# First tiles behind both norms of the second block taken from the unnormalised residual

## Chip, core and metric

The kernel runs on one core of one Trainium2 chip. The metric is the device time of one execution in microseconds (us). Three timed executions of the kernel before gave 1817.52 us as median (1816.81 to 1820.13).

## What is computed

Two transformer blocks in a row on a sequence of 512 tokens with 1024 channels, all in f32. The change touches the second block only:

```python
# second block; x is the first block's output behind its closing norm
shift1, scale1, gate1, shift2, scale2, gate2 = split(silu(c) @ w_ada + b_ada, 6)
h = rmsnorm(x, norm1_g) * (1 + scale1) + shift1
proj = h @ w_in                      # 24 tiles of 128 columns: "in2"
xc = causal_dwconv(x_rnn, conv_w, conv_b)          # tiles 0 to 9 of proj
...                                  # gated recurrence on xc, latent attention, merge
x = x + gate1 * (merged @ w_out)
h2 = rmsnorm(x, norm2_g) * (1 + scale2) + shift2
u = causal_dwconv(h2 @ w_up, ffn_conv_w, ffn_conv_b)   # 44 tiles: "up", tile m and tile 22+m are a pair
x = x + gate2 * ((silu(u_gate) * u_val) @ w_down)
```

With a scale s per channel, a factor r per token and a shift b per channel, (x * s * r + b) @ W is r * ((x * s) @ W) + b @ W. The last form needs r only behind the matrix product.

## The kernel before

Channels lie on the partitions and tokens in the free dimension, so one tile is 128 channels by 512 tokens. Every weight block is 128 by 128, and TensorE (PE) runs three 128x512 matmuls on it (lines 252 to 254), because each f32 operand is split into a high and a low half: whi*hi, whi*lo, wlo*hi. `proj` makes one output tile out of its blocks (8 for 1024 channels, so 24 matmuls). `proj2` makes two at once, k by k, 6 matmuls for each k, and is used where the operands come up one by one.

Weights stream in chunks of 8 blocks in the order in which PE uses them. SyncE (SP) loads a chunk into one of four `raw` buffers. ScalarE (ACT) makes the high half of a whole chunk (line 851), and VectorE (DVE) then the low half (line 1429); PE waits for the low half of a chunk before its first block. Both do that in `prep(b)`, which runs up to two chunks past block b. `start_of(name, m)` is `prep` at the first block of tile m. These calls stand between the other work of ACT and DVE, which do their instructions in the written order. `first` keeps, for a pair made by `proj2`, neighbouring numbers for its two tiles. Tile in2 0 begins at the start of a chunk; tile up 0 begins in the middle of one (its pair's k = 2 is the first to wait for a low half). Below, c0 to c6 are the chunks from the one in which up 0 begins, so c0 holds k = 0 and 1 of the first pair, c1 k = 2 to 5, and so on.

**The two norms.** Tiles HS[0..7] hold the residual. For each, ACT squares it (line 861) and DVE adds the squares (line 1443). PE sums over the channels with 128x1 matmuls (`total2`, `total3`, lines 278 and 284), DVE makes the variance, GpSimd (POOL) the power -1/2 (lines 2227 and 2399), DVE a diagonal of it (line 1451), PE spreads that over all partitions (`spread`, line 294). `modulated` then makes the operands: for each k DVE multiplies by scale and factor (line 1476), ACT adds the shift and rounds to the high half (line 1160 or 1373), DVE makes the low half (line 1481). Meanwhile PE runs `busy` matmuls of ones (line 290). The first norm is two in one (r1 closes block one, r12 is both together); the residual itself is also written back scaled (`x2`, line 1946).

**Behind the first norm** come the 24 in2 tiles. DVE convolves tiles 0 to 9 (`conv`, lines 1935 and 1937), and PE runs four short matmuls on each (`gate_rnn`, line 547), which wait for `conv(i)` and for ACT's `lru_i(i-1)` (line 1170).

**Behind the second norm** come the up pairs. For pair m ACT moves tile m out of its bank (line 1386), DVE does two steps of the convolution (2166, 2168), ACT the silu (1391), the same for tile 22+m (1393, then DVE), and DVE the product (2186). Each pair's `start_of` calls stand in between.

**The scales and shifts** come from `ada`: DVE multiplies each of 48 loaded rows of w_ada with silu(c) and sums (line 1849), beside the feed-forward of block one.

## Time and profile before

| what | us |
|---|---|
| median of three timed executions | 1817.52 |
| the profiled execution | 1816.73 |
| its span in the trace | 1814.9 |
| last matmul of tile pg 7 to first matmul of in2 0 | about 942.4 to 955.5 |
| last matmul of out2 7 to first matmul of up 0 | about 1426.0 to 1435.7 |

The times of the last two rows are positions in the span. The page of the profile shows each engine's share of the span, the timeline the instructions in order of time, and the chain of waits what released each step of the path that ended last. A matmul's duration in the timeline covers its passage through the array; the distance between two starts is what it costs in a row.

### The profile page before, as it was taken

What the parts mean: (1) busy time and instruction counts of PE and PEld (TensorE: products, weight loads), DVE (VectorE), ACT (ScalarE), POOL (GpSimd) and SP (SyncE); (2) the same over time, 40 slices, a digit from 0 to 9 for tenths busy, and PEclk for the clock granted to TensorE, in tenths of its full rate; (3) what the DMA queues carried; (4) which work ended last, traced back from release to release, by engine and by line L of the source; (5) the groups of instructions that cost most, each with busy time, mean ns of one, the idle gap of its engine ahead of it and who ended that gap; (6) DMA issues with size and microseconds to landing.
All of it is one profiled execution on the core that took longest, in us unless ns stands there. A gap on an engine that the chain in (4) does not pass through costs nothing.

```text
span 1814.9 us, 21224 instructions
## 1 busy us (share of the span) xinstructions
PE 1801.6 (99%) x8312; PEld 1439.0 (79%) x8312; DVE 1024.8 (56%) x1523; ACT 775.1 (43%) x1224; POOL 264.9 (15%) x349
## 2 busy tenths in 40 slices
PE   9999999999999999999999999999999999999998
PEld 7888888878887888888887688766668888888887
DVE  8754554756566544554468785255544665435543
ACT  6554454524344222222244756355643344324443
POOL 4766536200000000000001100322110000000000
PEclk9999999999999999999999999999999999999999
DMA  6222223134344545552332222412133233333331
GB/s 215 96 85 88 70 88 91 47 116 151 94 144 163 185 153 193 195 190 94 112 114 91 96 89 78 131 64 59 36 131 125 70 94 98 100 93 93 93 93 70
DMA packets 64259, 198.92 MB, mean 110 GB/s; under 512 B 7136, under 2 KB 11488, under 8 KB 64160
## 3 DMA queue, kind: packets, MB, share of 16 engines
q1 hardware_dynamic: 64160, 197.57, 33.5%
q8 instruction: 66, 1.08, 0.2%
q14 instruction: 33, 0.27, 0.1%
HBM read 189.15 MB, written 8.39 MB: 109 GB/s over the span
## 4 chain that ended last, share of the span: by engine, by line
PE 90%; issue 5%; ACT 2%; DVE 2%; DMA 0%; POOL 0%; SPq 0%; POOLq 0%; ACTq 0%; DVEq 0%
PE bank L252 27%; PE bank L254 26%; PE bank L253 26%; PE bank L656 2%; PE bank L671 1%; PE bank L686 1%; PE bank L298 1%; PE bank L341 1%; PE bank L357 1%; ACT whi L851 1%; PE bank L547 0%; DVE wlo L1429 0%; PE bank L387 0%; PE bank L378 0%; DMA raw<-wst 0%
## 5 line engine op out<-in xcount | busy, mean ns | idle before, releaser
L252 PE MATMUL bank<-tiler,whi 128*128 128x512 f32 x2260 | 905.9, 401 | 3.5 <-DVE tiler L1456 1.2
L254 PE MATMUL bank<-tiler,wlo 128*128 128x512 f32 x2260 | 891.9, 395 | 0.0
L253 PE MATMUL bank<-tiler,whi 128*128 128x512 f32 x2260 | 891.5, 394 | 0.0
L851 ACT ACTIVATE whi<-raw 128x1024 fp32r<-128x1024 f32 x284 | 298.9, 1054 | 546.3 <-PE bank L254 539.3
L252 PEld LDWEIGHTS bank<-tiler,whi 128*128 128x128 f32 x2260 | 426.1, 189 | 118.0 <-issue 18.7
L254 PEld LDWEIGHTS bank<-tiler,wlo 128*128 128x128 f32 x2260 | 425.5, 188 | 99.6
L253 PEld LDWEIGHTS bank<-tiler,whi 128*128 128x128 f32 x2260 | 426.1, 189 | 94.3 <-issue 1.0
L1429 DVE TENSOR_TENSOR wlo<-raw,whi 128x1024 fp32r<-128x1024 f32 x263 | 324.2, 1237 | 271.2 <-ACT whi L851 270.8
L2227 POOL TENSOR_TENSOR stat<-stat,scl 128x4 f32<-128x4 f32 x6 | 6.5, 1091 | 738.3 <-DVE stat L1923 427.2
L2166 DVE SCALAR_TENSOR_TENSOR tile<-bank,sm,tile 128x511 f32<-128x511 f32 x44 | 33.0, 750 | 97.9 <-ACT tile L1393 61.9
L2218 POOL TENSOR_TENSOR wlo<-raw,whi 128x1024 fp32r<-128x1024 f32 x21 | 49.8, 2373 | 219.4 <-ACT whi L851 219.4
L1456 DVE TENSOR_TENSOR tiler<-tile,tiler 128x512 fp32r<-128x512 f32 x109 | 73.9, 686 | 4.5 <-ACT tiler L1139 2.1
L861 ACT ACTIVATE tile<-tile 128x512 f32<-128x512 f32 x45 | 28.3, 630 | 101.0 <-DVE tile L2198 35.9
L1849 DVE CUSTOM_DVE_ANT_0 wide<-wide 128x1024 f32<-128x1024 f32 x48 | 58.5, 1220 | 0.0
L2079 DVE TENSOR_REDUCE stat<-bank 128x1 f32<-128x512 f32 (+1 forms) x64 | 31.3, 490 | 43.9 <-PE bank L658 42.8
L1283 ACT ACTIVATE wide<-bank,stat 128x512 f32<-128x512 f32 (+1 forms) x64 | 33.4, 525 | 44.6 <-DVE stat L2079 44.6
L656 PE MATMUL bank<-tile 96*128 96x384 f32 (+7 forms) x128 | 43.9, 450 | 0.4
L2198 DVE SCALAR_TENSOR_TENSOR tile<-bank,mod,tile 128x512 f32<-128x512 f32 x16 | 11.9, 751 | 55.7 <-PE bank L254 55.7
L1393 ACT ACTIVATE tile<-bank,sm 128x512 f32<-128x512 f32 x22 | 17.1, 779 | 53.3 <-PE bank L254 53.3
L1878 DVE TENSOR_TENSOR tile<-tile,bank 128x512 f32<-128x512 f32 x22 | 15.1, 688 | 42.8 <-PE bank L254 40.1
L1892 DVE TENSOR_TENSOR tile<-tile,bank 128x512 f32<-128x512 f32 x16 | 11.0, 687 | 47.2 <-PE bank L254 47.2
L1386 ACT ACTIVATE tile<-bank,sm 128x512 f32<-128x512 f32 x22 | 17.1, 779 | 44.1 <-PE bank L254 44.1
(372 smaller groups left out, 1597.2 us busy)
## 6 DMA issues: line engine op xcount, KB each, us to landing
raw<-wst SPq DMA_DIRECT2D x284, 512.0 KB, 3.6
wide<-wadaT SPq DMA_DIRECT2D x48, 512.0 KB, 3.5
tile<-xT SPq DMA_DIRECT2D x16, 256.0 KB, 5.3
spare<-tile SPq DMA_DIRECT2D x16, 256.0 KB, 2.0
tile<-spare SPq DMA_DIRECT2D x16, 256.0 KB, 6.3
out<-tile SPq DMA_DIRECT2D x8, 256.0 KB, 2.5
tile<-gblk SPq DMA_DIRECT2D x5, 256.0 KB, 4.8
us<-tile SPq DMA_DIRECT2D x4, 256.0 KB, 2.0
```

Of the source, the lines that this page charges most:

```text
L252: e.matmul(bank, whi[:, o:o + 128], hi, start=start, stop=False)
L253: e.matmul(bank, whi[:, o:o + 128], lo, start=False, stop=False)
L254: e.matmul(bank, wlo[:, o:o + 128], hi, start=False, stop=stop).then_inc(*sig("blk", n))
L656: e.matmul(bk[:, 0:w], F(QM[h % 2])[K, n * 128:(n + 1) * 128], F(KM[h % 2])[K, 0:w], start=True, stop=True, skip_group_check=True)
L851: e.activation(whi[:, c % NHL * W:(c % NHL + 1) * W], raw[:, c % NRAW * W:(c % NRAW + 1) * W], ACT.Copy).then_inc(*sig("hi", c))
L1283: e.activation(prob(h, n), B[3 + (n + 1) % 2][:, 0:w], ACT.Exp, bias=stat[:, ST_MM + z + n:ST_MM + z + n + 1], accum_out=stat[:, ST_MD + z ...
L1429: e.tensor_tensor(wlo[:, h:h + W], raw[:, c % NRAW * W:(c % NRAW + 1) * W], whi[:, h:h + W].bitcast(F32), SUB).then_inc(*sig("lov", c))
L1456: e.tensor_tensor(R(lo), src, R(hi).bitcast(F32), SUB).then_inc(*sig("oplo", name, k))
L1849: e.tensor_tensor_reduce(w, w, F(CR, 2), 1.0, 0.0, MUL, ADD, F(PART)[:, m:m + 1]).then_inc(*sig("ada", m))
L2079: e.tensor_reduce(stat[:, c:c + 1], B[3 + (n + 1) % 2][:, 0:(n + 1) * 128], AX, MAX, negate=True).then_inc(*sig("mmax", h, n))
L2166: then(e.scalar_tensor_tensor(out=F(t)[:, 1:512], in0=bk[:, 0:511], scalar=col("fcw", 44 + mt), in1=F(t)[:, 1:512], op0=MUL, op1=ADD))
L2218: e.tensor_tensor(wlo[:, h:h + W], raw[:, c % NRAW * W:(c % NRAW + 1) * W], whi[:, h:h + W].bitcast(F32), SUB).then_inc(*sig("log", c))
```

## The change

The first pair behind each norm (in2 0 and 1, up 0 and 22) is made from x * s, the residual times its scale, without factor and shift. ACT and DVE make the halves XS and XS2 of that as soon as each residual tile is there (`raw_lo`). The matmuls for sum and spread stand between the steps of that pair, and `busy` is gone. The second pair takes the normed operands. The first pair's banks are copied out by ACT behind all eight normed operands, multiplied by the factor on DVE, and given b @ W (a column) by ACT. The columns b @ W are four more rows of `ada` (48 to 51): their weights are columns of w_in and w_up, and the vector c is replaced by the shift, which SP writes to memory and reads back to all partitions (`load_shift`). `gate_rnn(i)` now stands one tile later, `x2` two tiles later, and `modulated` preps one chunk in the middle (k = 5) and not behind.

```diff
@@ tensor
-            busy(B[6], 8)
-            total2("r1", 51, B[4])
-            total2("r12", 52, B[5])
-            total3("r1", 56, B[4])
-            total3("r12", 58, B[5])
-            busy(B[6], 10)
-            spread("r12", 53, B[6])
-            spread("r1", 54, B[7])
-            busy(B[4], 5)
...
+            ba, bb = bank("raw", 0), bank("raw", 1)
+            for k in range(8):
+                e.wait_ge(*at("oplo", "xs", k))
+                proj("in2", 0, ba, XS, [k])
+                proj("in2", 1, bb, XS, [k])
+                if k == 3:
+                    total("r12", 52, B[4], 8)
+                if k == 5:
+                    spread("r12", 48, B[6])
+                if k == 6:
+                    total("r1", 72, B[5])
+            ba, bb = bank("conv", 2), bank("conv", 3)
+            proj2("in2", 2, ba, "in2", 3, bb, NN, "nn")
+            spread("r1", 30, B[7])
+            gate_rnn(0)
+            for m in range(4, 24):
...
-                if 2 <= m < 12:
-                    gate_rnn(m - 2)
+                if m < 13:
+                    gate_rnn(m - 3)
...
-            busy(B[7], 5)
-            total2("n3", 24, B[6])
-            total3("n3", 26, B[6])
-            busy(B[7], 8)
-            spread("n3", 25, B[7])
-            busy(B[6], 9)
-            p = 0
+            ba, bb = bank2(0, "raw2", 0), bank2(1, "raw2", 1)
+            for k in range(8):
+                e.wait_ge(*at("oplo", "xs2", k))
+                proj("up", 0, ba, XS2, [k])
+                proj("up", 22, bb, XS2, [k])
+                if k == 3:
+                    total("n3", 24, B[6])
+                if k == 5:
+                    spread("n3", 25, B[7])
+            p = 2
@@ scalar
+                e.activation(R(XS[m][0]), F(HS[m]), ACT.Copy, scale=scl[:, S_GF + m:S_GF + m + 1]).then_inc(*sig("ophi", "xs", m))
...
-            prep(first.get(("in2", 0), 0) + 8)
+                if k == 3:
+                    prep(first.get(("in2", 0), 0) + 8)
+            for i in range(2):
+                e.wait_ge(*made("in2", i))
+                e.activation(F(48 + i), B[i], ACT.Copy).then_inc(*sig("raw", i))
+            for i in range(2):
+                e.wait_ge(*at("rawn", i))
+                e.activation(F(48 + i), F(48 + i), ACT.Identity, bias=stat[:, 235 + i:236 + i]).then_inc(*sig("rawb", i))
@@ vector
-            def modulated(name, rb, w, ops, so, sh):
+            def modulated(name, rb, w, ops, so, sh, ahead):
                 for k in range(9):
+                    if k == 5:
+                        prep(ahead)
...
+                    if hf and m in (4, 5):
+                        ada(44 + m)
+                    if hf and m == 7:
+                        ada(50)
+                        ada(51)
...
+            def raw_lo(name, k, ops, so):
+                hi, lo = ops[k]
+                e.wait_ge(*at("ophi", name, k))
+                e.scalar_tensor_tensor(out=R(lo), in0=F(HS[k]), scalar=scl[:, so + k:so + k + 1], in1=R(hi).bitcast(F32), op0=MUL,
+                                       op1=SUB).then_inc(*sig("oplo", name, k))
...
+            modulated("nn", B[6], SILU, NN, S_GF, 0, first.get(("in2", 0), 0) + 8)
+            variance("r1", B[5], 1024, ST_R1)
+            for i in range(2):
+                e.wait_ge(*at("raw", i))
+                e.tensor_tensor(F(48 + i), F(48 + i), B[6], MUL).then_inc(*sig("rawn", i))
+            diagonal("r1", ST_R1, 30)
@@ sync
+            def load_shift(x, so):
+                e.wait_ge(*at("mod") if x == 0 else at("ada", 49))
+                e.dma_start(shd[x], mod[:, so:so + 8]).then_inc(*sig("shd", x, by=16))
+                e.wait_ge(*at("shd", x))
+                e.dma_start(F(CR, 2), shd[x].rearrange("p k -> (p k)").unsqueeze(0).to_broadcast([128, 1024])).then_inc(
+                    *sig("shr", x, by=16))
```

The same copy, product and addition stand behind the second norm (raw2, rawn2, rawb2).

TensorE behind the second norm, before: the spread (L294), the ones, then the pair up 0 and 22 on normed operands; of each k the first matmul is shown where it waits.

```order
L294 MATMUL bank<-tile,ones 128x512 [waits s_dg]
L290 MATMUL bank<-ones 128x128 x9
L252 MATMUL bank<-tiler,whi 128x512 [waits s_oplo,s_residual]
...
L252 MATMUL bank<-tiler,whi 128x512 [waits s_lov,s_oplo]
...
L252 MATMUL bank<-tiler,whi 128x512 [waits s_residual]
...
L252 MATMUL bank<-tiler,whi 128x512 [waits s_lov]
```

The s_lov waits shown are those for c1 (k = 2 of the first pair) and, behind up 1's start, for c3. After, from the spread, which now stands ahead of k = 6 of the raw pair, into the pair up 1 and 23:

```order
L296 MATMUL bank<-tile,ones 128x512 [waits s_dg]
L254 MATMUL bank<-tiler,whi 128x512 [waits s_lov,s_oplo]
...
L254 MATMUL bank<-tiler,whi 128x512 [waits s_oplo,s_residual]
...
L254 MATMUL bank<-tiler,whi 128x512 [waits s_lov,s_oplo]
...
L254 MATMUL bank<-tiler,whi 128x512 [waits s_lov,s_oplo]
...
L254 MATMUL bank<-tiler,whi 128x512 [waits s_copied]
```

The three s_lov waits are for c2 (raw k = 6), c3 (k = 2 of the next pair) and c4 (its k = 6); up 2 follows. Before, c4 was first needed in the middle of up 23, behind the whole of up 1.

ScalarE at the same place, before: the eight high halves of the operands, a weight chunk (c3), the moves of pair 0, then c4.

```order
L1373 ACTIVATE tiler<-tile,mod 128x512 [waits s_w] x8
L851 ACTIVATE whi<-raw 128x1024 [waits s_blk,s_w1]
L1386 ACTIVATE tile<-bank,sm 128x512 [waits s_blk]
L1391 ACT_TABLE_LOAD
L1391 ACTIVATE tile<-tile 128x512 [waits s_cv_g]
L1393 ACTIVATE tile<-bank,sm 128x512 [waits s_blk]
L851 ACTIVATE whi<-raw 128x1024 [waits s_blk,s_w2]
```

After:

```order
L1393 ACTIVATE tiler<-tile,mod 128x512 [waits s_w] x4
L862 ACTIVATE whi<-raw 128x1024 [waits s_blk,s_w1]
L1393 ACTIVATE tiler<-tile,mod 128x512 [waits s_w] x4
L1398 ACTIVATE tile<-bank 128x512 [waits s_blk] x2
L1401 ACTIVATE tile<-tile,stat 128x512 [waits s_lru_dve] x2
L1416 ACTIVATE tile<-tile,sm 128x512 [waits s_copied]
L1421 ACT_TABLE_LOAD
L1421 ACTIVATE tile<-tile 128x512 [waits s_cv_g]
L1426 ACTIVATE tile<-tile,sm 128x512 [waits s_copied]
L862 ACTIVATE whi<-raw 128x1024 [waits s_blk,s_w2]
L1416 ACTIVATE tile<-bank,sm 128x512 [waits s_blk]
L1426 ACTIVATE tile<-bank,sm 128x512 [waits s_blk]
L862 ACTIVATE whi<-raw 128x1024 [waits s_blk,s_w3]
```

(The last four are c4, the two moves of pair 1 and c5; their products lie between.) The chunk c4 stands behind four new instructions and pair 0's moves, and c5 behind pair 1's moves; before, c5 stood between the two moves of pair 1.

TensorE and VectorE at the first gate_rnn, after: the spread of r1, the gate's matmuls (L540), then in2 4.

```order
L296 MATMUL bank<-tile,ones 128x512 [waits s_dg]
L540 MATMUL bank<-tile 64x512 [waits s_gw,s_lru_dve]
L540 MATMUL bank<-tile 64x512 x3
L254 MATMUL bank<-tiler,whi 128x512 [waits s_lov,s_copied]
```

```order
L1480 TENSOR_SCALAR stat<-bank 128x4 [waits s_tot]
L1981 TENSOR_TENSOR tile<-tile,bank 128x512 [waits s_copied] x2
L1484 TENSOR_TENSOR tile<-ident,stat 128x512 [waits s_rstd]
L1462 TENSOR_TENSOR wlo<-raw,whi 128x1024 [waits s_hi]
L1991 TENSOR_SCALAR tile<-tile,sm 128x512 [waits s_copied]
L1993 SCALAR_TENSOR_TENSOR tile<-tile,sm 128x511 [waits s_dve]
```

`conv(0)` (from L1991), for which the gate waits, stands behind the factor's products, r1's diagonal and a weight chunk.

## Rows read from the trace of the kernel before

**Rows 1.** The page: span, share of TensorE, chain of waits by engine.
```profile
span 1814.9 us, 21224 instructions
...
PE 90%; issue 5%; ACT 2%; DVE 2%; DMA 0%; POOL 0%; SPq 0%; POOLq 0%; ACTq 0%; DVEq 0%
```

**Rows 2.** Busy time by stretch: window, length, PE PEld DVE ACT POOL (x), clock, DMA.
```profile
800.00:900.00 100.00, 100.00 (x432) 81.09 (x431) 43.54 (x59) 25.26 (x32) 0.00 (x0) 1.00 0.34 112
```

**Rows 3.** Chain of waits at the first norm: start us, us, what.
```profile
942.76 1.79 PE bank L290 x16
944.55 1.68 PE bank L278 x16
...
948.01 3.97 PE bank L290 x20
951.98 0.88 PE bank L294 x2
952.96 0.76 DVE tile L1476
...
955.50 0.48 PE bank L252
```

**Rows 4.** Timeline at the first norm: start us, us, engine, line, operands, [idle before].
```profile
944.15 0.69 DVE L1915 TENSOR_TENSOR tile<-tile 128x512 f32<-128x512 f32 x1
...
949.53 0.69 DVE L1451 TENSOR_TENSOR tile<-ident,stat 128x512 f32<-128x512 f32 x1 [1.12 <-POOL stat L2227]
```

**Rows 5.** Timeline of DVE ahead of the first gate_rnn: a chunk, conv(0), conv(1).
```profile
968.10 1.23 DVE L1429 TENSOR_TENSOR wlo<-raw,whi 128x1024 fp32r<-128x1024 f32 x1 [2.62 <-ACT whi L851]
969.24 0.81 DVE L1935 TENSOR_SCALAR tile<-bank,sm 128x512 f32<-128x512 f32 x1
...
972.32 0.80 DVE L1935 TENSOR_SCALAR tile<-bank,sm 128x512 f32<-128x512 f32 x1
```

**Rows 6.** Timeline of PE, gate_rnn(0) and gate_rnn(1).
```profile
972.46 1.09 PE L547 MATMUL bank<-tile 64*64 64x512 f32 x8
979.26 1.09 PE L547 MATMUL bank<-tile 64*64 64x512 f32 x8
```

**Rows 7.** What PE waited for from 960 to 1120 us: us, times, longest.
```profile
PE bank L547 <- ACT tile L1170: 0.4, 1, 0.4
```

**Rows 8.** DVE groups by form: busy us, mean ns, idle before.
```profile
L1935 DVE TENSOR_SCALAR tile<-bank,sm 128x512 f32<-128x512 f32 x10 | 8.1, 805 | 0.0
...
L2086 DVE TENSOR_SCALAR wide<-wide,stat 128x512 f32<-128x512 f32 x16 | 7.8, 487 | 0.6
```

**Rows 9.** Timeline at the second norm, DVE, PE and ACT.
```profile
1433.25 1.41 DVE L1476 SCALAR_TENSOR_TENSOR tile<-tile,scl,bank 128x512 f32<-128x512 f32 x2 [1.22 <-PE bank L294]
...
1435.69 0.47 PE L252 MATMUL bank<-tiler,whi 128*128 128x512 f32 x1 [0.47 <-DVE tiler L1481]
...
1437.56 0.73 ACT L1373 ACTIVATE tiler<-tile,mod 128x512 fp32r<-128x512 f32 x1 [0.60 <-DVE tile L1476]
...
1438.76 0.75 DVE L1481 SCALAR_TENSOR_TENSOR tiler<-tile,mod,tiler 128x512 fp32r<-128x512 f32 x1
```

**Rows 10.** Timeline of ACT: the move of up 0 out of its bank.
```profile
1446.42 0.78 ACT L1386 ACTIVATE tile<-bank,sm 128x512 f32<-128x512 f32 x1 [1.91 <-PE bank L254]
```

**Rows 11.** Timeline of DVE: the low half of chunk c4 behind pair 0.
```profile
1452.32 1.22 DVE L1429 TENSOR_TENSOR wlo<-raw,whi 128x1024 fp32r<-128x1024 f32 x1
```

**Rows 12.** Short windows: columns as in Rows 2; the clock stands ahead of DMA share.
```profile
948.20:948.40 0.20, 0.20 (x4) 0.20 (x2) 0.17 (x2) 0.00 (x0) 0.00 (x0) 0.50 1.08 430
951.40:951.60 0.20, 0.20 (x3) 0.20 (x3) 0.00 (x0) 0.00 (x0) 0.00 (x0) 0.55 0.00 0
1811.00:1812.00 1.00, 0.00 (x0) 0.00 (x0) 0.00 (x0) 0.00 (x0) 0.00 (x0) 0.87 1.04 404
```

**Rows 13.** Timeline of PE: the last matmuls of the kernel.
```profile
1806.44 2.82 PE L829 MATMUL bank<-ident,tile 128*128 128x128 f32 x24
```

**Rows 14.** DMA issues of w_ada's rows: count, KB each, us to landing.
```profile
wide<-wadaT SPq DMA_DIRECT2D x48, 512.0 KB, 3.5
```

More of the change, by code:

```diff
@@ L548, in gate_rnn @@
                     ins.then_inc(*sig("lru_g", i, c))
-            ba, bb = bank("conv", 0), bank("conv", 1)
-            proj2("in2", 0, ba, "in2", 1, bb, NN, "nn")
-            for m in range(2, 24):
+            ba, bb = bank("raw", 0), bank("raw", 1)
[14 more added lines that the diff above has]
+            for m in range(4, 24):
                 if m < 10:
@@ L1373, in scalar @@
                 e.activation(R(N1[k][0]), F(CU[k % 3]), ACT.Identity, bias=mod[:, 24 + k:25 + k]).then_inc(*sig("ophi", "n3", k))
-            prep(first.get(("up", 0), 0) + 8)
+                if k == 3:
+                    prep(first.get(("up", 0), 0) + 8)
+            for i in range(2):
+                e.wait_ge(*made("up", 22 * i))
+                e.activation(F(70 + i), B[i], ACT.Copy).then_inc(*sig("raw2", i))
+            for i in range(2):
+                e.wait_ge(*at("rawn2", i))
+                e.activation(F(70 + i), F(70 + i), ACT.Identity, bias=stat[:, 237 + i:238 + i]).then_inc(*sig("rawb2", i))
             p = 0
@@ L1909, in vector @@
                     sums(m - 2)
+                    raw_lo("xs", m - 2, XS, S_GF)
                 if m == 7:
@@ L1916, in vector @@
             prep(first.get(("in2", 0), 0))
[L1917 to L1934 removed]
+            sums(7)
+            e.wait_ge(*at("acc", "r12", 7))
+            e.wait_ge(*at("acc", "r1", 7))
+            e.scalar_tensor_tensor(out=F(52), in0=F(72), scalar=1e-6, in1=F(52), op0=MUL, op1=ADD).then_inc(*sig("acc", "r12", 8))
+            raw_lo("xs", 6, XS, S_GF)
+            raw_lo("xs", 7, XS, S_GF)
+            e.wait_ge(*at("tot", "r12"))
+            e.tensor_scalar(stat[:, ST_R12:ST_R12 + 4], B[4][:, 0:4], 1.0 / 1024, 1e-12, MUL, ADD).then_inc(*sig("var", "r12"))
+            diagonal("r12", ST_R12, 48)
+            e.wait_ge(*at("rb", "r12"))
+            modulated("nn", B[6], SILU, NN, S_GF, 0, first.get(("in2", 0), 0) + 8)
+            variance("r1", B[5], 1024, ST_R1)
+            for i in range(2):
+                e.wait_ge(*at("raw", i))
+                e.tensor_tensor(F(48 + i), F(48 + i), B[6], MUL).then_inc(*sig("rawn", i))
+            diagonal("r1", ST_R1, 30)
+            def conv(i):
+                x, bk = F(XC[i]), B[i % 4] if i >= 2 else F(48 + i)
+                if i >= 2:
+                    e.wait_ge(*made("in2", i))
+                else:
+                    e.wait_ge(*at("rawb", i))
                 then(e.tensor_scalar(x, bk, col("convw", 30 + i), col("convb", i), MUL, ADD))
@@ L2161, in vector @@
             e.wait_ge(*at("rb", "n3"))
-            modulated("n3", B[7], CU, N1, S_N2, 24)
-            prep(first.get(("up", 0), 0) + 8)
+            modulated("n3", B[7], CU, N1, S_N2, 24, first.get(("up", 0), 0) + 8)
+            for i in range(2):
+                e.wait_ge(*at("raw2", i))
+                e.tensor_tensor(F(70 + i), F(70 + i), B[7], MUL).then_inc(*sig("rawn2", i))
             def conv2(t, bk, mt):
@@ L2488, in sync @@
             e.dma_start(F(CR, 2), cT[:, :]).then_inc(*sig("cT", by=16))
-            for m in range(48):
+            for m in range(51):
                 if m >= 3:
```

87 lines of the change are left out of this document (50 added, 37 removed).

## Prediction

> **What bounds the kernel.** The page gives TensorE (PE) nearly the whole chain of waits [rows 1], so only what lengthens or shortens PE's own row of work counts. In a dense stretch PE starts 432 matmuls in 100 us [rows 2]: 0.2315 us each, 0.695 for a weight block (3), 1.39 for one k of a pair (6), 5.56 for a tile (24), 11.1 for a pair. Then the chain at the first norm: from 942.8 to 955.5 PE runs only ones, sums and spreads, and ends in a wait for the first operand [rows 3]: 12.9 us without a tile. At the second the same runs from 1426.3 to 1435.8: 9.5 us. The change puts tiles into both gaps. What it wins is read from the next things that PE needs behind them: operands, weight halves, conv(0).
>
> **First norm.** The raw pair starts at 942.6. Its operands are in time: h_pg 7 was ready at 944.84 [rows 4], and behind it DVE has a chunk (1.14 us from start to start [rows 5]), two additions, the joining of the two sums and two low halves (0.6 to 0.7 each), so k = 6 and 7 are there by 949.4, long before PE reaches them. The total for r12 stands at 942.6 + 4 x 1.39 = 948.2, when DVE has just ended the joined sum (948.0): no wait. It takes 0.84 (half of 1.68 for two [rows 3]). Variance, POOL's power and the diagonal take about 2 us behind it [rows 4] and are hidden by k = 4 and 5. Spread at 951.8 (0.86: half of what is left of two spreads [rows 3]), k = 6, second total, k = 7: the pair ends at 956.3. The factor reaches DVE at 952.95 (in the trace 1.15 behind the spread's start); call that w. The first operand is whole at w + 2.3 (952.96 to 955.26 [rows 3]), so 955.3; the rest follow 1.32 apart, PE takes one in 1.39. The chunk put into modulated at k = 5 moves the later ones by 1.14: operand 4 is ready at w + 8.7 = 961.7, PE comes at 961.9. So in2 2 and 3 run from 956.3 to 967.4 unbroken.
>
> Then the spread of r1 (to 968.3) and gate_rnn(0), which needs conv(0). DVE ends modulated's last low half at w + 12.2 = 965.2, then makes two products (to 966.5) and r1's diagonal; ACT adds the two columns until 967.3, makes the high half of a chunk until 968.3, and DVE, behind it, the low half: conv(0) starts at 969.4. It took 3.1 [rows 5] and now reads a tile where it read a bank, so its first step may cost 0.49 as in the second row of [rows 8] and not 0.81: done at 972.3. **PE stands from 968.3 to 972.3.** In the trace the first gate started at 972.46 with three tiles done [rows 6]; now at 972.35 with four. That wins 5.56 + 0.1 = 5.7. The gates' pitch of 6.8 [rows 6] stays: chunk and lru_i are up to a tile early. The wait of 0.4 ahead of the last gate [rows 7] should go, since ACT's chunk there no longer waits for PE: 6.1 in all.
>
> **Second norm.** Raw pair from 1426.3, the total at 1431.8 to 1432.7, spread at 1435.5, w = 1436.6, pair ends at 1439.1; the first operand is there at w + 2.3 = 1438.9. So far the 9.5 us would be down to the sum and the spread, 1.7. But up 0 starts in the middle of a chunk, and the order rows show s_lov at k = 2 and at k = 6 of the next pair. Chunk c3 stands in modulated at k = 5 on DVE: behind low half 3 (in the trace 1438.76 - 1433.25 = 5.5 behind w [rows 9]) plus 0.66, and its high half stands behind ACT's k = 3 (4.3 behind w [rows 9]) plus 0.65 + 1.05; so it is whole at w + 7.4 = 1444.0. PE wants it at 1439.1 + 2 x 1.39 = 1441.9 and resumes at 1444.2: 2.3 lost. Chunk c4 is wanted after k = 5, at 1449.8. On ACT and DVE it stands behind all of modulated (low half 7: w + 12.2), two copies, two products, two additions, and the moves of pair 0. The products start at 1448.75, the second addition ends at 1450.8, the first move starts then; in the trace from that start to the end of c4's low half 1452.32 + 1.22 - 1446.42 = 7.1 passed [rows 10, 11]; from tiles I take 7.0: 1457.7. **PE stands from 1449.8 to 1457.8**, 8.0. Chunk c5 is wanted two k and four blocks later, at 1463.4. It now stands behind the moves of pair 1, which wait for up 1 (its last block ends 2.1 + 0.2 behind the resume, 1460.1); two moves, two convolutions, the silu and the product as in pair 0 bring c5's low half to 1467.3, PE resumes at 1467.4: 4.0 more. Eight blocks later, at 1473.0, PE is at the block that it reached in the trace at 1435.8 + 44 x 0.695 = 1466.4. **The second norm loses 6.6**, though its gap is gone: 2.3 + 8.0 + 4.0 + 1.7 = 16.0 (16.1 unrounded) for 9.5. Behind it the chunks are ahead again.
>
> **The clock.** The ones are gone, and there are now three stands of 3.9, 8.0 and 4.0 us. The granted clock was 0.50 (1.2 GHz) from 948.2 to 951.5 [rows 12], after 3.5 us of 128x1 matmuls, and fell at 1811.7, 2.5 us behind the last matmul at 1809.3 [rows 12, 13]. A matmul costs twice its time at that level, so a resume that meets the whole 3.4 us of it loses 1.6, one that meets none loses 0. I take 1.0 for each stand, near the middle: 3.0. In the second norm the slow start also holds up 1 and with it c5; that is inside the 1.0.
>
> The Trainium skill (TensorE: Matmul & The Clock Gate, Why this matters for your kernels) asks for matmul bursts without idle gaps of some microseconds, or the clock goes to its lower level; by that rule every one of the three stands costs, and the sum is the upper one of this part. The end of the kernel agrees with it, the stands of under 1 us in this trace don't test it.
>
> **The rest.** raw_lo and the XS copies are 32 instructions of 0.6 to 0.75 us beside pg and out2, where DVE is under half busy [rows 2]: nothing. Four ada rows (1.2 each) stand on DVE in the last fd tiles. Their rows land 3.5 us behind the issue [rows 14]; the shift goes out and comes back through memory. The nearest row for each way is that 3.5, so 7 us between fd 5's end and ada(50) behind fd 7, 15 us later. SP stands meanwhile, but its chunks are issued two further than ACT needs. Two more ada ahead of pg's second chunk leave that 0.6 us early. Bounds for all this: 0 to 1.
>
> **Sum.** -6.1 + 6.6 + 3.0 = +3.5 on 1816.73: 1820.2 for the profiled execution. That one lay 0.8 below the median, so the median becomes 1817.5 + 3.5 = **1821.0**.
>
> **Rivals.**
> *The halves come in time* (faster). If c4 and c5 were made before PE wants them, the second norm would win 9.5 - 1.7 = 7.8 less 0.8 for operand 4, and with -6.1 and 1.0 for the one clock fall the sum is -12: 1805.5. Against it stands the order: c4 is the instruction behind pair 0's moves on ACT and on DVE. The Trainium skill (TensorE: Matmul & The Clock Gate, Part 1) calls the queues of ScalarE and VectorE strictly first in, first out; by that rule nothing passes the moves, and the trace has no row where one did.
> *The clock holds.* No resume meets the lower level: -6.1 + 6.6 = +0.5, 1818.0. For it: no such stand is in the trace before its end. Against: that end.
> *Slower by more.* The clock takes its full price three times, 4.8, and the moves of pair 1 wait for an up 1 that runs at half speed (nine matmuls, 2.1): 0.5 + 6.9 = +7.4, 1824.9. It decides when the 8 us stand resumes just after the clock fell.
> *The shift comes late.* ACT waits for ada(51) ahead of XS 0 and DVE in ada(50): from 11 us more than I take, each us would be lost. Nothing in the trace reaches such a time.
>
> **How the numbers follow.** Forecast 0.62, halves in time 0.07, clock holds 0.16, slower by more 0.13, shift late 0.02. About 0.2%, 3.6 us, can be told from no change: the bounds are 1813.9 and 1821.2. The forecast's own range, with the price of the stands open by 0.6 each, conv(0) by 0.3 and ada by 1, is 1819 to 1823.5 and lies across the upper bound, nearly in halves (0.31 and 0.31). So faster 0.09 (0.07, and 0.02 of the clock case), same 0.45, slower 0.46. The range takes in the clock that holds and most of the slower case: 1816.5 to 1824.8.
>
> **What would show it.** Right: PE idle ahead of gate_rnn(0) (about 4 us, released by conv(0)), ahead of k = 2 of up 1 and 23 (2.3), of its k = 6 (8) and of up 2's fifth block (4), each released by a low half of weights; windows of clock 0.50 behind them; in2 4 starting near 973.6. Wrong: a first gate near 968.3, no wait at k = 6, or a wait for ada(50).

## The result, and the profile after

The changed kernel takes 1824.34 us (median of seven, 1822.76 to 1825.88) against 1818.01 (1816.81 to 1820.13): ratio 1.0039, 95% interval 1.0029 to 1.0048. Its profiled execution took 1824.03 us with a span of 1822.2, where the one before took 1816.73 with 1814.9: **7.3 us more**. The forecast was 1821.0, 3.5 more; its range held the time.

The page of the changed kernel, span and chain of waits by engine (as [rows 1]). TensorE's share of the chain reads 94% where it was 90%, and the kernel is slower all the same. The difference says nothing of the change: the chain before puts one piece of 87.66 us, from 1342.61, down as `issue`, in a stretch in which PE is busy without a pause in both kernels:

```profile
span 1822.2 us, 21066 instructions
...
PE 94%; DVE 3%; ACT 2%; issue 0%; DMA 0%; SPq 0%; ACTq 0%
```

What PE waited for over the whole span (line waited for: us in total, times, longest). The wait for conv(0) (L1993) is new. For low halves of weights (L1462) there was one wait of 0.5 before, which is still there, and three are new. The third line is the kernel's first operand, the last is [rows 7] again:

```profile
PE bank L254 <- DVE wlo L1462: 12.7, 4, 6.5
PE bank L540 <- DVE tile L1993: 3.7, 1, 3.7
PE bank L254 <- DVE tiler L1545: 1.9, 1, 1.9
...
PE bank L540 <- ACT tile L1189: 0.4, 1, 0.4
```

PE's timeline at the first norm, of what is no tile (start us, us, what, [idle before]). The total stands four k behind the pair's start, so the pair started at 949.53 - 24 x 0.2315 = 943.97; from the spread of r1 PE goes to the first gate, where it stands (as [rows 6]):

```profile
949.53 0.95 PE L273 MATMUL bank<-ones,tile 128*128 128x1 f32 x8
...
968.88 1.02 PE L296 MATMUL bank<-tile,ones 128*128 128x512 f32 x2
973.60 1.20 PE L540 MATMUL bank<-tile 64*64 64x512 f32 x8 [3.70 <-DVE tile L1993]
981.92 1.09 PE L540 MATMUL bank<-tile 64*64 64x512 f32 x8
```

The chain of waits through that stand (start us, us, what), which answers [rows 5]: product, ACT's addition and its high half, the low half on DVE, then conv(0) in four steps:

```profile
966.56 0.61 DVE tile L1981
...
967.82 0.71 ACT tile L1180
968.53 0.96 ACT whi L862
...
969.51 1.23 DVE wlo L1462
970.73 0.47 DVE tile L1991
...
972.80 0.76 DVE tile L1993
...
973.60 1.20 PE bank L540 x8
```

The same at the second norm, PE's timeline. The first row is the total, so the pair started at 1428.92 - 5.56 = 1423.36. The three last rows are the stands ahead of k = 2 and k = 6 of up 1 and 23 and of up 2's fifth block:

```profile
1428.92 0.95 PE L273 MATMUL bank<-ones,tile 128*128 128x1 f32 x8
...
1441.19 0.47 PE L254 MATMUL bank<-tiler,whi 128*128 128x512 f32 x1 [2.03 <-DVE wlo L1462]
1455.07 0.77 PE L254 MATMUL bank<-tiler,whi 128*128 128x512 f32 x1 [6.51 <-DVE wlo L1462]
1466.45 0.80 PE L254 MATMUL bank<-tiler,whi 128*128 128x512 f32 x1 [3.69 <-DVE wlo L1462]
```

Busy time in short windows (us, PE PEld DVE ACT POOL with counts, then the clock). The clock is at 0.50, the lower level of 1.2 GHz, behind three of the four stands, shown here, and from 1466.0 to 1469.4 at the last one ([rows 12] show the level once between the norms' ones and once at the end):

```profile
976.00:977.00 1.00, 1.00 (x3) 0.74 (x3) 1.00 (x2) 0.96 (x3) 0.03 (x1) 0.50 0.00 0
...
1443.00:1444.00 1.00, 1.00 (x4) 0.71 (x4) 1.00 (x3) 0.72 (x1) 0.00 (x0) 0.50 0.71 279
...
1457.00:1458.00 1.00, 1.00 (x4) 0.81 (x3) 0.00 (x0) 0.00 (x0) 0.00 (x0) 0.50 0.81 328
```

**Where the 7.3 us come from.** Each trace is cut at two places: where PE ends the tiles ahead of the first norm and ahead of the second. Where the raw pair is there its start is worked out as above. "To the end" ends at the start of the last group of transposes [rows 13]; the rest is 8.5 to 9.4 us in all traces.

| kernel | first norm reached | to the second norm | to the end | span |
|---|---|---|---|---|
| before | 942.60 | 483.66 | 380.18 | 1814.9 |
| changed | 943.97 (+1.4) | 479.39 (-4.3) | 390.12 (+9.9) | 1822.2 |

So 1.4 was lost ahead of both places, where the change only adds side work, 4.3 won at the first norm, 9.9 lost at the second, and 0.3 lies behind the last transposes. The 1.4 begins at the kernel's first tile: PE waited 1.93 us for its first operand (0.71 before) and then started matmuls 0.43 us apart for 3.4 us, where 0.23 is usual. That left it 2.3 us behind; 0.9 came back between 28 and 38 us, where two waits of the kernel before (0.68 and 0.20) had nothing left to wait for. PE's timeline at the first tile:

```profile
8.27 0.63 PE L254 MATMUL bank<-tiler,whi 128*128 128x512 f32 x1 [1.93 <-DVE tiler L1545]
```

### The profile page after: what moved, and what is told of

Same layout as the page of the kernel before. It is cut to its first block, busy times and chain, and to the rows that moved or that the text cites. A ratio compares the mean times of both kernels' runs of the same rounds, so it can differ in the third digit from the quotient of the medians.

```text
span 1822.2 us, 21066 instructions
## 1 busy us (share of the span) xinstructions
PE 1794.4 (98%) x8198; PEld 1429.3 (78%) x8198; DVE 1042.1 (57%) x1554; ACT 788.1 (43%) x1248; POOL 266.8 (15%) x349
## 4 chain that ended last, share of the span: by engine, by line
PE 94%; DVE 3%; ACT 2%; issue 0%; DMA 0%; SPq 0%; ACTq 0%
PE bank L254 28%; PE bank L256 28%; PE bank L255 28%; PE bank L663 2%; PE bank L693 1%; PE bank L678 1%; PE bank L300 1%; PE bank L343 1%; PE bank L359 1%; DVE wlo L1462 1%; DVE tiler L1516 1%; DVE tile L1511 1%; PE bank L540 1%; PE bank L389 0%; PE bank L380 0%
## 5 line engine op out<-in xcount | busy, mean ns | idle before, releaser
L1462 DVE TENSOR_TENSOR wlo<-raw,whi 128x1024 fp32r<-128x1024 f32 x263 | 323.6, 1235 | 265.1 <-ACT whi L862 264.8
L1887 DVE CUSTOM_DVE_ANT_0 wide<-wide 128x1024 f32<-128x1024 f32 x52 | 63.3, 1218 | 0.0
```

The source lines that it names most:

```text
L1462: e.tensor_tensor(wlo[:, h:h + W], raw[:, c % NRAW * W:(c % NRAW + 1) * W], whi[:, h:h + W].bitcast(F32), SUB).then_inc(*sig("lov", c))
L1887: e.tensor_tensor_reduce(w, w, F(CR, 2), 1.0, 0.0, MUL, ADD, to).then_inc(*sig("ada", m))
```

## The experiments

The same cuts for all of them, as differences from the trace of before, and the ratio to the kernel before on the same chip:

| kernel | first norm | to the second | to the end | ratio (95%) |
|---|---|---|---|---|
| changed | +1.4 | -4.3 | +9.9 | 1.0039 (1.0029 to 1.0048) |
| changed, second trace | +0.2 | -4.2 | +11.5 | 1.0045 (1.0031 to 1.0058) |
| side work alone | -0.2 | 0.0 | 0.0 | 0.9999 (0.9990 to 1.0008) |
| first norm alone | +0.3 | -3.4 | 0.0 | 0.9979 (0.9970 to 0.9988) |
| second norm alone | +0.4 | +0.1 | +11.5 | 1.0062 (1.0048 to 1.0076) |
| stands filled | +1.7 | -5.8 | +6.8 | 1.0004 (0.9995 to 1.0013) |
| chunks earlier | +0.3 | -3.3 | -2.2 | 0.9974 (0.9965 to 0.9983) |
| gates later | +0.5 | +6.9 | +10.9 | 1.0101 (1.0085 to 1.0116) |
| both of these | -0.1 | +6.3 | -3.7 | 1.0025 (1.0016 to 1.0033) |
| chunks earlier, bank later | -0.2 | -5.8 | -6.7 | 0.9946 (0.9934 to 0.9959) |
| gates and sigmoids later | +0.5 | -3.5 | +12.6 | 1.0043 (1.0031 to 1.0056) |
| the four together | +0.9 | -5.0 | -6.7 | 0.9943 (0.9930 to 0.9957) |
| and the chunks at conv | +0.3 | -9.4 | -6.7 | 0.9922 (0.9909 to 0.9936) |

The cuts come from one traced execution each, the ratios from four to eleven timed ones.

**A slower pace of PE in four traces.** In the second trace of the changed kernel, in *second norm alone* and in *gates and sigmoids later*, PE ran 0.4% slower from its last stand to the end of the tiles, with the granted clock at 1.00 and no wait: the last 450 weight blocks took 314.3 us, in all other traces 313.0. So 1.3 us of the +11.5, +11.5 and +12.6 are neither stands nor low clock. With the stands filled the same pace holds from about 560 us to the first norm and makes about 1.5 of that trace's +1.7. One window of the changed kernel's first and second trace (as [rows 2]; 432 and 430 matmuls in 100 us):

```profile
1600.00:1700.00 100.00, 100.00 (x432) 81.09 (x431) 48.01 (x57) 34.05 (x42) 0.00 (x0) 1.00 0.31 96
1600.00:1700.00 100.00, 100.00 (x430) 80.43 (x429) 48.03 (x57) 34.00 (x42) 0.00 (x0) 1.00 0.31 94
```

### Side work alone

The kernel before with the four rows of `ada` (1.2 us each on DVE) and the shift's trips, whose results nobody reads. The copies and low halves of x * s (XS, `raw_lo`) are not in it:

```
+                    if hf and m in (4, 5):
+                        ada(44 + m)
+                    if hf and m == 7:
+                        ada(50)
+                        ada(51)
...
+            load_shift(0, 0)
...
+            load_shift(1, 24)
```

> The kernel before, with only the four ada rows, the two trips of the shift through memory and their waits added; norms, tiles and gates as before, so nothing reads the four sums. The changed kernel's trace reaches the first raw pair at 943.95 us where the trace before reached the norm at 942.60, 1.35 later, and the first place where they differ is the kernel's start: PE waits 1.93 us for its first operand instead of 0.71 and then runs its first eight matmuls at the lower clock. Theory: that is spread from one execution to the next (when the first transfers land) and no part of the change; this kernel is then within 1 us of before (1817 to 1819), and DVE ends the last fd tile's work without PE waiting in front of pg. Rival: the additions cost it, through DVE in front of pg's second chunk or through the loads; then this kernel is 1.3 us or more slower, and its PE shows a wait between 830 and 945 us that the trace before has not.

1817.35 us against 1818.09. No cut differs by more than 0.2. The 0 that the prediction took for these holds, and the 1.4 does not come from them. For XS and `raw_lo` beside pg the next kernel stands, which has them and reaches the first norm 0.3 late.

### First norm alone, second norm alone

The change, with the hunks of the second norm (TensorE's raw pair of up 0 and 22, its sums, copies and moves) or those of the first taken back, so that one norm is as changed and the other as before.

> Only the first norm's part of the change (with all four ada rows); the second norm as before. The recorded working gives -6.1 for the first norm and +1.0 for the clock, -5.1: 1813. The trace of the changed kernel shows -4.3 between the place where PE reaches the first norm and the place where it reaches the second (4.0 us of stand in front of gate_rnn(0), then a full 3.4 us at 1.2 GHz, 1.6 lost, and the wait of 0.4 in front of the last gate still there): 1813.7. Rival, that the first norm gives nothing and the two parts interact: 1818 or more. All of it shifts up by 1.3 if the start's loss belongs to the change.

> Only the second norm's part of the change; the first norm as before. The recorded working gives +6.6 and +2.0 for two falls of the clock: 1826.6. The trace of the changed kernel shows +10.2 between the place where PE reaches the second norm and the end: 1828.2. Rival: the late weight halves come only because the first norm's part lets PE arrive 3 us earlier; then this kernel would show shorter stands and lie near 1822. Stands expected: 2.0 in front of k = 2, 6.5 in front of k = 6 of up 1 and 23, 3.7 in front of up 2's fifth block.

1813.35 and 1829.69 against 1818.09: -4.7 and +11.6 by medians, -2.8 and +12.9 by spans. The parts add up to the whole (-0.0021 and +0.0062 make +0.0041, the changed kernel has +0.0039), and each part leaves the other's stretch alone within 0.1 us. The stands are those of the changed kernel, though in the second kernel PE arrives 3.4 us later; its PE timeline:

```profile
1444.59 0.47 PE L254 MATMUL bank<-tiler,whi 128*128 128x512 f32 x1 [2.03 <-DVE wlo L1449]
1458.46 0.77 PE L254 MATMUL bank<-tiler,whi 128*128 128x512 f32 x1 [8.06 <-DVE wlo L1449]
1469.84 0.50 PE L254 MATMUL bank<-tiler,whi 128*128 128x512 f32 x1 [3.27 <-DVE wlo L1449]
```

The pair started at 1426.76 here and at 1423.36 in the changed kernel. Counted from there PE resumes at 17.83, 31.70 and 43.08 us, in the changed kernel at 17.83, 31.71 and 43.09. So the resumes are set by the work on ACT and DVE behind the norm, and not by when PE arrives; the rival, that only PE's earlier arrival makes the halves late, is out. That the second stand is 8.06 here and 6.51 there is the clock: here it held behind k = 2, PE reached k = 6 1.5 us sooner, and waited that much longer.

### Stands filled

Products of ones into a bank that nobody reads, as long as the waits:

```
+            busy(B[4], 15)
             gate_rnn(0)
...
+                        for k in range(8):
+                            busy(B[6], {2: 8, 6: 34}.get(k, 0))
...
+                        if m == 2:
+                            busy(B[6], 15)
```

> The changed kernel with 128x128 products of ones into a bank that nobody reads put where PE stands: 15 in front of gate_rnn(0), 8 in front of k = 2 and 34 in front of k = 6 of up 1 and 23, 15 in front of the fifth block of up 2. Each takes 0.23 us at the full clock, so they end about when the wait ends; the waits themselves stay. It tells the clock's price apart from the stands. Theory: the clock stays at 1.00; 1.6 comes back behind gate_rnn(0); behind k = 2 nothing, since the wait for k = 6 grows by the same 1.6; 1.6 behind k = 6, with up 1's end and so the chunk behind its moves earlier; 1.3 behind up 2's fifth block: 4.5 in all, 1819.8 against the changed kernel's 1824.3. Rival, that the clock's price is as small as the recorded working has it (1.0 each): 3.0 or less comes back, 1821.3 or more. Rival, that the resumes cost their time for another reason than the clock: nothing comes back.

1818.46 against 1818.09, 5.9 less than the changed kernel's median. Busy time and clock of PE in windows behind the four places (us, PE (x), clock):

```profile
973.00:979.00 6.00, 5.65 (x31) 1.00 0.01 3
1442.00:1446.00 4.00, 4.00 (x21) 1.00 0.17 69
1454.00:1460.00 6.00, 6.00 (x29) 1.00 0.32 87
1463.00:1469.00 6.00, 5.63 (x25) 1.00 0.57 178
```

The clock holds in all of them, and the two stretches read -5.8 and +6.8 where the changed kernel reads -4.3 and +9.9. The clock's part is thus 1.5 at the first norm and 3.2 at the second, 4.7 in its first trace; without it the two norms come near the prediction's sums (-6.1 and +6.6). PE resumes for up 2's fifth block 41.3 behind the pair's start, where it was 43.1: up 1 at full speed lets pair 1's moves and the chunk behind them begin earlier. As expected nothing comes back behind k = 2: ones fill 7.75 us ahead of k = 6 instead of a stand of 6.51.

### Chunks earlier

At the second norm the chunks c3 to c9 each one place earlier on ACT and DVE (shown for ACT, the same on DVE):

```
+AHEAD = {1: (16, 24), 2: (16, 16)}
...
-            prep(first.get(("up", 0), 0))
+            prep(first.get(("up", 0), 0) + 8)
...
-                    prep(first.get(("up", 0), 0) + 8)
+                    prep(first.get(("up", 0), 0) + 16)
+            prep(first.get(("up", 0), 0) + 24)
...
+            prep(first.get(("up", 0), 0) + 32)
...
-                        start_of("up", m)
+                        prep(first.get(("up", m), 0) + AHEAD.get(m, (0, 0))[0])
```

> The changed kernel with the weight chunks of the second norm made earlier on ScalarE and VectorE, nothing else moved: c3 ahead of the norm's variance, c4 in c3's old place at modulated's k = 5, c5 behind modulated, c6 ahead of pair 0's moves, and c7 to c9 each one place earlier in the moves of pairs 1 and 2. The order is the cause, by the recorded working and by the changed kernel's trace: the three stands behind the low halves (2.0, 6.5, 3.7) go, and with them the two falls of the clock that cost anything (1.6 and 1.3). A new wait of up to 2 us is possible in front of up 3, whose bank comes free only when pair 1's first convolution is done. So 1.6 more than the three stands and the clock may give back less than all of 16.7: 1824.3 - 16.7 + 0 to 2 = 1807.6 to 1809.6. Rival: the chunks are late for want of engine time, not by their order; then VectorE's own work in front of the norm's factor or of the operands becomes the wait, stands of 8 us or more stay between 1424 and 1480, and the time stays above 1816.

1811.93 against 1816.76, where 1807.6 to 1809.6 was expected. All three stands are gone: from +9.9 to -2.2. The order was their cause, and DVE had the time. The expected range was missed by the new wait, 3.12 us instead of up to 2, and by the clock, which fell behind it for 3.4 us. PE's timeline:

```profile
1462.45 0.67 PE L255 MATMUL bank<-tiler,whi 128*128 128x512 f32 x1 [3.12 <-DVE tile L2235]
```

and DVE's, the second convolutions of up 1 and of up 23:

```profile
1458.66 0.75 DVE L2235 SCALAR_TENSOR_TENSOR tile<-bank,sm,tile 128x510 f32<-128x510 f32 x1
...
1461.56 0.75 DVE L2235 SCALAR_TENSOR_TENSOR tile<-bank,sm,tile 128x510 f32<-128x510 f32 x1
```

up 3 writes the bank that the first of them frees at 1459.4. PE waited for the other, at 1462.3, since it asks for a pair's two banks at once.

### The second bank later

```
-                    ba, bb = bank2(p, "cv_g", m), bank2(p + 1, "cv_u", m)
+                    ba = bank2(p, "cv_g", m)
...
                         proj("up", m, ba, N1)
+                        bb = bank2(p - 1, "cv_u", m)
                         proj("up", 22 + m, bb, N1)
```

> The kernel with the chunks moved earlier, and TensorE asks for the bank of up 22 + m only when up m is done, instead of ahead of up m. In the trace without this edit PE stood 3.1 us in front of up 3 until pair 1's second convolution was done (1462.3), though the bank that up 3 itself writes was free at 1459.4, and the clock then fell for 3.4 us. Theory: this stand shrinks to 0.5 or less and the clock does not fall: 3.1 + 1.6 less, 4.7 less than the kernel with the chunks alone (0.9974 of before), so 0.9948 of before, 1808.5. Rival: VectorE is behind for want of time and not by this order; then the wait moves to the bank of up 25 or to a low half behind it, and 2 us or less come back.

1807.56 against 1816.88, 0.9946 where 0.9948 was expected. A wait of 0.15 is left there. The second stretch is 6.7 shorter than before; the prediction's rival *the halves come in time* had 9.5 - 1.7 - 0.8 = 7.0 for it. The trace is of the fastest of five executions (1804.37), and in it the clock did not fall at gate_rnn(0) either.

### Gates later, with and without their sigmoids

```
-            gate_rnn(0)
...
-                if m < 13:
-                    gate_rnn(m - 3)
+                if m < 14:
+                    gate_rnn(m - 4)
```

> The changed kernel with each gate of the first norm one tile later (gate_rnn(0) behind in2 4 instead of behind in2 3), nothing else moved. It tells the price of the stand in front of gate_rnn(0). Theory: the stand of 3.7 is covered by in2 4 (5.6 us long), the clock does not fall there, and the gates' pitch of 6.8 leaves the last gate 1.3 us later than now, which nobody waits for: 3.7 + 1.6 = 5.3 less, 1819.0. Rival: work behind the last gate (the scan, the attention's first latent tiles) hangs on the gates and waits by as much; then less than 2 us comes back and a wait shows between 1030 and 1060 us.

> The edits of both kernels above on the changed kernel: chunks earlier at the second norm and gates one tile later at the first. If the two are independent: 1807.6 to 1809.6 less 5.3 = 1802.3 to 1804.3, against 1818.0 before. Rival, that they meet in a common limit (VectorE between the norms): no better than the better of the two.

Both expectations missed: 1834.99 against 1816.76, 11 us slower than the changed kernel, and 1820.00 against 1816.76 with the chunks earlier too, where 1802.3 to 1804.3 was expected. The first one's rival looked for a wait between 1030 and 1060 and one came (2.9 us, until 1041.5), but it had no loss in it. The stand in front of gate_rnn(0) went and others came. What was waited for from 965 to 985 us in the first of them:

```profile
ACT tile L1184 <- PE bank L540: 8.3, 1, 8.3
...
PE bank L254 <- DVE wlo L1461: 5.7, 2, 4.7
DVE wlo L1461 <- ACT whi L861: 2.7, 2, 1.5
```

gate_rnn(0) now stands directly ahead of in2 5. ACT waits 8.3 us for it at the sigmoid, and the high half of the chunk for in2 5 (not in2 4, as the expectation below has it) is queued behind that sigmoid; DVE waits for the high half and PE for DVE's low half, so that chunk can't be made until the gate is done. Two more waits, 2.9 and 2.1 us, follow between 985 and 1100 us, and with them two more falls of the clock. The chunks at the second norm give in the kernel with both what they gave alone (-3.7 there, -2.2 alone, with no fall of the clock behind the bank).

With ScalarE's part moved along:

```
-                if 3 <= m <= 12:
-                    lru_sigmoids(m - 3)
-                if 4 <= m <= 13:
-                    lru_tanh(m - 4)
+                if 4 <= m <= 13:
+                    lru_sigmoids(m - 4)
+                if 5 <= m <= 14:
+                    lru_tanh(m - 5)
```

> The changed kernel with each gate one tile later, as in the kernel that lost 11 us, and with ScalarE's sigmoids and tanh of the gates one tile later too. In the trace of that kernel ScalarE waited for gate_rnn(0) (8.3 us) with the high half of the chunk that TensorE needed for in2 4 queued behind it. Theory: that order was the whole loss; with both moved the stand of 3.7 in front of gate_rnn(0) and the 1.6 of the clock go: 5.3 less than the changed kernel, 1819, 1.0010 of before. Rival: the chunks of tiles 4 to 6 are late by themselves, because VectorE makes three convolutions in a row ahead of them; then a wait of 1 to 4 us for a low half stays between 968 and 985, and the time is 1821 or more.

> All four edits on the changed kernel: chunks earlier and the second bank asked for later at the second norm, gates and their sigmoids one tile later at the first. If the parts add up: 0.9948 less 5.3 us, 0.9919 of before, 1803.3. Rival, a common limit of VectorE between the norms: not below the better of the two alone.

1824.60 against 1816.88, and 1806.71 for the four edits together. The big loss is gone, so ScalarE's order was its cause; but the first one's rival was right that two low halves stay late (1821 or more), and the four edits together are hardly better than without the gates (0.9943 against 0.9946, with 0.9919 expected). PE's timeline in the kernel with the four edits:

```profile
970.45 0.47 PE L255 MATMUL bank<-tiler,whi 128*128 128x512 f32 x1 [0.98 <-DVE wlo L1466]
980.29 0.47 PE L255 MATMUL bank<-tiler,whi 128*128 128x512 f32 x1 [3.00 <-DVE wlo L1466]
```

And DVE's. conv(0), conv(1) and conv(2) stand in a row from 970.23; the first line is the last three steps of conv(2), the second the low halves of two chunks behind it:

```profile
976.70 2.31 DVE L1997 SCALAR_TENSOR_TENSOR tile<-bank,sm,tile 128x511 f32<-128x511 f32 x3
978.93 3.45 DVE L1466 TENSOR_TENSOR wlo<-raw,whi 128x1024 fp32r<-128x1024 f32 x2
```

A stand of 3.7 had become stands of 1.0 and 3.0.

### The chunks at conv

```
+            prep(first.get(("in2", 0), 0) + 16)     (ahead of the raw copies on ACT, of variance on DVE)
...
+            prep(first.get(("in2", 0), 0) + 24)     (behind the additions on ACT, behind conv(0) on DVE)
...
-            spread("r1", 30, B[7])
+                if m == 4:
+                    spread("r1", 30, B[7])
```

> The kernel with all four edits, and at the first norm a fifth: the chunk for in2 4 made ahead of the raw pair's two products, additions and the norm's last diagonal, the chunk for in2 5 between conv(0) and conv(1), and the spread of r1 put behind in2 4. The trace without this edit has two waits for low halves, 1.0 in front of in2 4 and 3.0 in front of in2 5, since three convolutions stood ahead of two chunks on VectorE. Theory: it is this order: both go, no new wait longer than 0.5 comes up to gate_rnn(0), 4.0 less than that kernel's 0.9943 of before: 0.9921, about 1803. Rival: VectorE has no time to give in this stretch (it made conv(0) to conv(2) without a pause), so the wait only moves, to the gates (conv(0) later than in2 4's end at 975) or to the chunk for in2 6, and 1 us or less comes back.

1801.65 against 1815.95, 0.9922 where 0.9921 was expected. What PE waited for over the whole span has no stand of a chunk over 0.5 us left, and conv(0) is not in it:

```profile
PE bank L255 <- DVE tiler L1496: 1.2, 2, 0.9
...
PE bank L255 <- DVE wlo L1469: 0.8, 2, 0.5
```

This kernel beats both: 14.3 us (0.78%) faster than before, and by the ratios 1.2% (21 us) faster than the change as made.

### The changed kernel once more

> The changed kernel once more, unedited, for a second trace. In its first trace PE waited 1.93 us for the kernel's first operand and the clock then fell for 3.4 us, so that PE reached the first norm 1.37 us later than in the trace before. None of the eleven kernels with the same start that were traced since shows that fall (their waits there are 0 to 1.7 us). If it is chance: no low clock in the first 15 us, the first norm reached by 942.4 to 943.1, and a span of 1820 to 1822. If it belongs to the change: the fall is there again and the span is 1822 or more. The same code at the second norm has cost between 9.9 and 12.6 us in four traces, by how long the clock stayed low behind the stands: a value in or near that range is expected.

1824.63 against 1816.76. PE waited 1.5 us at the start and the clock did not fall; the first norm was reached at 942.79. So the same kernel runs without the fall at the start too, and of the thirteen traces with no such fall eleven are of kernels made from the change. The span was 1822.8 nevertheless, above the 1820 to 1822 expected, as the stretch behind the second norm took 1.6 more, 1.3 of it by the slower pace. The order and the resumes are the same, counted from the pair's start at 1422.30:

```profile
1440.12 0.47 PE L254 MATMUL bank<-tiler,whi 128*128 128x512 f32 x1 [2.03 <-DVE wlo L1462]
1454.01 0.76 PE L254 MATMUL bank<-tiler,whi 128*128 128x512 f32 x1 [8.06 <-DVE wlo L1462]
1465.38 0.68 PE L254 MATMUL bank<-tiler,whi 128*128 128x512 f32 x1 [3.42 <-DVE wlo L1462]
```

## Why the prediction was right or wrong

The forecast had +3.5, most of it at the second norm, and the likeliest verdict was drawn nearly in halves between "within 0.2%" and "slower". It is slower, by 0.39%. The order of events was right; one term of the sum, the clock's 3.0, was too small, and that decided the verdict. By medians the change costs 6.3, by the first trace 7.3, of which 1.4 belongs to the start.

**First norm, -6.1.** In place: pair at the expected pitch, no wait for the total, one stretch of tiles up to the spread of r1, 24.9 us behind the start of the pair (24.8 expected), the gate 29.6 behind it (29.75). The first step of conv(0) took 541 ns from its tile, where 490 was taken from [rows 8]. Without the clock the stretch gave 5.8 (stands filled; the kernel with the bank edit gives the same). The 0.3 that is missing is the last gate's wait of 0.4, which was to go and is there. The reason given, that ACT's chunk there would no longer wait for PE, is true of the chunk and wins nothing: before, ACT waited 3.0 for PE at a chunk (until 1020.23), now it waits 3.0 at the sigmoid behind it, for gate_rnn(7) (until 1023.84). Either way that sigmoid starts 1.1 behind the start of gate_rnn(7), and from it ACT works without a pause for 12.8 us until the last gate may start: two gates' sigmoids, a tanh, five exponentials (3.18), two table loads (1.28 each), a chunk, a move and a square. PE is there 0.4 sooner. With the sigmoids moved too, the same 0.4 stands ahead of gate_rnn(8).

**Second norm, +6.6.** Right to 0.2 us without the clock: 6.8 with the stands filled. Resumes at 17.83, 31.7 and 43.1 behind the pair's start, where 17.9, 31.4 and 41.1 were expected. Stands of 2.0, 6.5 and 3.7 for 2.3, 8.0 and 4.0. The second is shorter because the clock's loss behind k = 2 lies inside it: DVE sets that resume, so a slow PE in front of it costs nothing. The third resume is 2.0 late: 0.3 from the second, and the rest from nine matmuls of up 1 at half speed, which move pair 1's moves and the chunk behind them. With the stands filled that resume came at 41.3, which shows it. Between the second and the third resume a slow PE costs its full price.

**The clock, +3.0.** This is the step that failed. Three stands at 1.0 each were summed; against the kernel with the stands filled, the clock cost 1.5 + 3.2 = 4.7 in the first trace. The 3.2 are nine matmuls of up 1 at half speed (an estimate of 1.8, from starts 0.43 and 0.23 us apart) and the rest, 1.4, behind up 2's fifth block. Over the five traces that have these stands the second norm's part is 3.2 to 4.6 (9.94 - 6.76 to 12.62 - 6.76 - 1.28, the slower pace taken off where it was), and the first norm's 0 to 2.4. The prediction had the nine matmuls and put them "inside the 1.0" without a price of their own. The rival *slower by more* had this mechanism, full price and up 1 at half speed, and its 1824.9 is the nearest number to the 1824.34 measured, at a chance of 0.13. That it came so near is in part luck: its clock term of 6.9 is above both traces of the changed kernel (4.7 and 5.1). A fall met in full was in the forecast's own rows: [rows 12] show one in a stretch of small matmuls, and no row showed a stand whose resume met none of it, so 1.0 as "near the middle" had no row behind it. The rival *the clock holds*, at 0.16, did not come true for the changed kernel; with ones in the stands the clock does hold, and the time is 1818.46 where it had 1818.0.

The rule of the Trainium skill (TensorE: Matmul & The Clock Gate, Why this matters for your kernels) that idle gaps of some microseconds cost the clock was the better guide: the stand at the first norm met a low clock in four traces of five, those ahead of k = 6 and of up 2's fifth block in all five that have them, and the sum by it was the upper one.

**The rest, 0.** Right within the noise: side work alone is 0.9999 of before, and with XS and `raw_lo` too the first norm is reached 0.3 late. Each of the shift's trips took 2.3 and 4.0 us, 6.3 together, where 7 was the bound:

```profile
wide<-shd SPq DMA_DIRECT2D x2, 512.0 KB, 4.0
shd<-mod SPq DMA_DIRECT2D x2, 4.0 KB, 2.3
```

**What was in no term.** The 1.4 at the kernel's start, where the clock fell in none of the other traces. It is part of the span's +7.3. The second trace has +7.8 without it: 1.0 from the norms without the clock, 5.1 from the clock (1.6 + 3.5), 1.3 from the slower pace, and 0.5 at the two ends.

What stays open: what starts the slower pace of PE, and how many of the timed executions had it; and why the same stand meets the low clock in one execution and not in another. The two traces that reached the first norm 1.7 and 0.9 late are accounted for: the first by that pace, the second by 0.4 at the first tile and 0.5 more of a wait at 29 us (1.23 for 0.68).

## What to carry to other kernels

Work that fills a gap on the bound engine also shifts every feeder's deadline; list what that engine needs next (weight halves, banks, the first consumer) and where each stands in its producer's queue, since here no engine lacked time and moving chunks by a place or two turned +6 us into -14. When a step is moved on one engine, move its partner on the other engines' queues too: the gate moved without its sigmoid cost 11 us. Ask for a bank where it is written, not a pair ahead, and put ones into a stand that can't be removed.

## What was not expected of the hardware

**The same stand costs the clock nothing, 1.5 or 2.4 us.** PE stood 3.7 us in front of gate_rnn(0) in five traces with the same code at that norm. PE's timelines of three of them, gate_rnn(0) and gate_rnn(1): the changed kernel has them 8.32 us apart (shown above), the one with the first norm alone 9.17, the one with the bank edit 6.81, the undisturbed pitch of [rows 6]:

```profile
972.53 1.98 PE L540 MATMUL bank<-tile 64*64 64x512 f32 x8 [3.70 <-DVE tile L1975]
981.70 1.09 PE L540 MATMUL bank<-tile 64*64 64x512 f32 x8
```

```profile
972.08 1.09 PE L541 MATMUL bank<-tile 64*64 64x512 f32 x8 [3.69 <-DVE tile L1998]
978.89 1.09 PE L541 MATMUL bank<-tile 64*64 64x512 f32 x8
```

PE's windows of these two (us, PE (x), clock): in the first the clock is already low while PE stands, in the second it never falls.

```profile
971.00:972.00 1.00, 0.00 (x0) 0.50 0.00 0
972.00:973.00 1.00, 0.47 (x4) 0.50 0.03 8
973.00:975.00 2.00, 2.00 (x9) 0.50 0.03 8
```

```profile
972.00:973.00 1.00, 0.92 (x8) 1.00 0.00 0
```

The low stretches ahead of the last transposes last, in all traces, 3.4, 6.8 or 10.2 us. A stand's price is therefore a spread (0 to 2.4 us here for 3.7), not a value, and one trace of one kernel doesn't give it. The Trainium skill (TensorE: Matmul & The Clock Gate, Part 1: The HAM clock gate) says that one kernel meets a differing number of slow matmuls from run to run; the traces agree, and show it in the middle of a kernel as well as at its start.

**The clock fell behind the start in one trace of fourteen**, after a wait of 1.9 us there; in the others these waits were 0 to 1.7 us and it held.

**PE has two paces at the full clock.** In four traces of fourteen a weight block took 0.7000 us instead of 0.6972, for hundreds of microseconds, with no wait and the clock at 1.00. The slower pace began at or behind a wait or stand (about 560 us in one trace, behind the stands of the second norm in three) and cost 1.3 to 1.5 us. Nothing tried here shows its cause.
